# The recurrent rounds of an RWKV-7 and dilated-attention trunk: every PE step in 64x64 quadrants, and a new order of the steps after the fifth inverse level

## What is computed

```python
def step(state, inp):                       # per head of 64, 16 heads, 512 tokens
    r_t, w_t, k_t, v_t, a_t, b_t = inp
    sa = einsum('bhij,bhj->bhi', state, a_t)
    state = state * w_t + sa[..., None] * b_t + v_t[..., None] * k_t
    return state, einsum('bhij,bhj->bhi', state, r_t)
```

## Time and profile before

| | us |
|---|---|
| median of 3 runs | 1778.16 (1777.97 to 1778.27) |
| the profiled execution | 1777.27 |
| its span, first to last instruction | 1775.5 |
| PE busy | 1742.2 (98%) |
| weight loads busy | 1351.5 (76%) |
| DVE / ACT / POOL busy | 904.0 / 742.5 / 202.0 |
| granted PE clock | 1.0 throughout, save the first slice |
| rounds 0 to 7 of the recurrence | about 133 to 454 us from the start |

### The profile page before, as it was taken

One profiled execution on the slowest core, in us unless ns is written; L12 is line 12 of the kernel. 1 busy time (PEld: TensorE's weight loads), 2 busy tenths in 40 slices (PEclk: granted clock), 3 DMA queues, 4 the chain that ended last, 5 costly groups with the idle time before them and its releaser, 6 DMA issues.

```text
span 1775.5 us, 35844 instructions
## 1 busy us (share of the span) xinstructions
PE 1742.2 (98%) x15388; PEld 1351.5 (76%) x15388; DVE 904.0 (51%) x1567; ACT 742.5 (42%) x1285; POOL 202.0 (11%) x172
## 2 busy tenths in 40 slices
PE   7999999999999999999999999999999999999999
PEld 2746666666478888888888888888887788888887
DVE  6825555554454444333556656655656544444321
ACT  6434444432243222222565665565655532222211
POOL 0033344431100000000111111111110000000000
PEclk9999999999999999999999999999999999999999
DMA  4321222231133223333322222322222233333332
GB/s 128 99 64 61 88 68 68 66 104 62 60 96 95 95 95 96 106 95 95 104 81 89 84 83 73 85 82 83 84 84 72 72 95 95 95 98 101 98 95 95
DMA packets 58453, 155.00 MB, mean 87 GB/s; under 512 B 6503, under 2 KB 23447, under 8 KB 58296
## 3 DMA queue, kind: packets, MB, share of 16 engines
q1 hardware_dynamic: 58200, 152.63, 27.7%
q10 hardware_dynamic: 96, 0.07, 0.0%
HBM read 150.51 MB, written 11.61 MB: 91 GB/s over the span
## 4 chain that ended last, share of the span: by engine, by line
PE 92%; DVE 4%; ACT 2%; issue 1%; DMA 1%; POOL 1%; SPq 0%; ACTq 0%; DVEq 0%; POOLq 0%
PE bank L618 89%; PE bank L621 2%; DVE f L2278 1%; DVE f L2193 0%; DVE r L2107 0%; ACT f L1684 0%; ACT r L1369 0%; DMA f<-xT 0%; ACT f L1686 0%; DMA f<-stream 0%; DMA f<-const 0%; DVE r L1785 0%; DVE f L1796 0%; DVE f L1809 0%; DVE f L1837 0%
## 5 line engine op out<-in xcount | busy, mean ns | idle before, releaser
L618 PE MATMUL bank<-r 128*128 128x512 f32 x5424 | 1253.4, 391 | 2.4 <-DVE r L2107 1.0
L618 PEld LDWEIGHTS bank<-r 128*128 128x128 f32 x5424 | 1012.6, 188 | 221.2 <-issue 6.2
L618 PE MATMUL bank<-f 64*64 64x64 f32 (+6 forms) x9532 | 457.1, 279 | 24.8 <-issue 5.2
L1785 DVE TENSOR_TENSOR r<-f,r 128x1024 fp32r<-128x1024 f32 x222 | 283.9, 1279 | 362.6 <-ACT r L1369 362.3
L618 PEld LDWEIGHTS bank<-f 64*64 64x64 f32 (+3 forms) x9532 | 291.3, 138 | 183.7 <-issue 112.3
L1369 ACT ACTIVATE r<-f 128x1024 fp32r<-128x1024 f32 x222 | 232.4, 1048 | 146.3 <-PE bank L618 141.5
L2465 POOL TENSOR_TENSOR r<-f,r 128x512 fp32r<-128x512 f32 x48 | 66.9, 1394 | 807.6 <-ACT r L1673 807.6
L1652 ACT ACTIVATE r<-f 128x512 fp32r<-128x512 f32 x44 | 27.8, 632 | 215.6 <-DVE f L2146 215.6
L2176 DVE TENSOR_TENSOR f<-bank,f 128x512 f32<-128x512 f32 x72 | 56.1, 778 | 74.9 <-PE bank L618 72.2
L1684 ACT ACTIVATE f<-bank,f 128x512 f32<-128x512 f32 x48 | 33.0, 688 | 101.5 <-PE bank L618 100.8
L1649 ACT ACTIVATE f<-f 128x512 f32<-128x512 f32 x44 | 27.8, 632 | 110.5 <-DVE f L2136 110.5
(11 more groups left out here) (117 smaller groups left out, 926.2 us busy)
## 6 DMA issues: line engine op xcount, KB each, us to landing
f<-stream SPq DMA_DIRECT2D x246, 512.0 KB, 3.6
bias_copies<-bias_rows SPq DMA_DIRECT2D x6, 1536.0 KB
f<-xT SPq DMA_DIRECT2D x16, 256.0 KB, 4.4
f<-lora_out SPq DMA_DIRECT2D x16, 128.0 KB, 6.2
f<-bias_copies SPq DMA_DIRECT2D x64, 32.0 KB, 2.4
f<-bias_copies SPq DMA_DIRECT2D x32, 64.0 KB, 2.1
outT<-f SPq DMA_DIRECT2D x8, 256.0 KB, 4.5
f<-const SPq DMA_DIRECT2D x1, 576.0 KB, 3.7
```

What stands on the lines that cost most here:

```text
L618: return nc.tensor.matmul(out, lhsT, rhs, start=start, stop=stop, skip_group_check=True)
L1785: TT(r(lo_at(q), 1024), f(O_RAW + panel_of(q) % RAW * 1024, 1024), rf(hi_at(q), 1024), ALU.subtract).then_inc(s["w_lo"], 1)
```

## The change

PE's transposes and the value product become 64x64 products in all four quadrants (`flip_corners`), which go to banks 0 and 1 as one tensor `sides`, read by one ACT copy that spans both. Removal and b are flipped together, behind one signal. The variance sum moves from bank 0 to bank 7. All sixteen projection chunks are quartered. The order of PE's list after level 5 changes for rounds that have a pair behind them, and DVE's list with it. The core of the diff:

```diff
-        banks = [... psum_tensor(f"bank{i}", [P, 512], F32) for i in range(8)]
+        sides = ctx.enter_context(nc.psum_tensor("sides", [P, 1024], F32))
+        banks = [sides[:, 0:512], sides[:, 512:1024]]
+        banks += [... psum_tensor(f"bank{i}", [P, 512], F32) for i in range(2, 8)]
-        QUARTERED = (0, 3, 4, 6, 7, 9, 10, 11, 12, 13, 14, 15)
         def quartered(k, step):
-            return 0 <= k < NHP and step in QUARTERED
+            return 0 <= k < NHP
-        SIDE = {0: [("b_tr", 0), ("akv", 0), ("bonus", 1), ("var", -1),
+        SIDE = {0: [("v_tr", 0), ("b_tr", 0), ("akv", 0), ("k_tr", 0), ("bonus", 1),
                     ("first", 1), ("bsc", 1), ("ksc", 1), ("w", 2), ("g", -1)],
-                1: [("kk", 1), ("v_tr", 0), ("a_tr", 0), ("k_tr", 0), ("first", 1), ("bsc", 1), ("ksc", 1),
-                    ("a", 2)]}
+                1: [("kk", 1), ("first", 1), ("bsc", 1), ("ksc", 1), ("a", 2)]}
             def variance_ready(hp):
-                fill(0, "var", hp)
+                pe.wait_ge(s["y_sb"], hp + 1)
+            def flip_corners(at, off, by):
+                for q in range(NT):
+                    for e in range(2):
+                        for h in range(2):
+                            last = mm(banks[h][CH * e:CH * (e + 1), at + q * HD:at + (q + 1) * HD],
+                                      half(off(q) + e * CH, h), half(O_CON + by + h * HD, h))
+                return last
             def value_flip(hp):
-                for q in range(NT):
-                    last = mm(banks[1][:, q * P:(q + 1) * P], f(vin(hp) + q * P, P), con(C_CENTRE))
-                last.then_inc(s["v_tr"], 1)
+                flip_corners(0, lambda q: vin(hp) + q * P, C_CENTRE).then_inc(s["v_tr"], 1)
-            def removal_flip(hp):
...
-            def b_flip(hp):
...
+            def removal_and_b_flip(hp):
+                fill(0, "b_tr", hp)
+                pe.wait_ge(s["ar_a"], hp + 1)
+                flip_corners(0, lambda q: chunk(O_AR, hp, 2 * P, q, 0), C_ID)
+                pe.wait_ge(s["bt"], hp + 1)
+                flip_corners(4 * HD, lambda q: chunk(O_BT, hp, P, q, 0), C_ID).then_inc(s["b_tr"], 1)
             def k_flip(hp):
-                    last = flip(banks[1][:, q * P:(q + 1) * P], f(chunk(O_KT, hp, P, q, 0), P))
+                flip_corners(0, lambda q: chunk(O_KT, hp, P, q, 0), C_ID).then_inc(s["k_tr"], 1)
@@ PE's list @@
-                project(k, 8)
-                if here:
-                    next_inverse(k, 5)
-                    project(k, 9)
-                    solve(k)
-                if after:
-                    first_inverse(k + 1)
-                if not here:
-                    project(k, 9)
-                project(k, 10)
-                if here:
-                    transitions(k)
-                project(k, 11)
-                if after:
-                    b_scores(k + 1)
-                project(k, 12)
-                if here:
-                    readout(k)
-                if after:
-                    k_scores(k + 1)
-                project(k, 13)
+                if here and after:
+                    first_inverse(k + 1)
+                    next_inverse(k, 5)
+                    project(k, 8)
+                    solve(k)
+                    b_scores(k + 1)
+                    project(k, 9)
+                    transitions(k)
+                    project(k, 10)
+                    project(k, 11)
+                    readout(k)
+                    project(k, 12)
+                    k_scores(k + 1)
+                    project(k, 13)
+                elif here:
...
+            def flipped(at):
+                return sides[:, :].rearrange("p (h q n) -> p h q n", h=2, n=HD)[:, :, at * NT:(at + 1) * NT, :]
             def keep_removal(hp):
-                side(1, (s["a_tr"], hp + 1), bc(f(O_YY, 2 * S), (S, 2), (P, NT), (1, HD)),
-                     in_=banks[1][:, :].rearrange("p (q h n) -> p h q n", q=NT, h=2), scale=-1.0)
+                act.wait_ge(s["b_tr"], hp + 1)
+                A(bc(f(O_YY, 2 * S), (S, 2), (P, NT), (1, HD)), flipped(0), ACT.Copy, scale=-1.0)
             def keep_b(hp):
-                side(0, (s["b_tr"], hp + 1), f(O_BTOK))
+                side(0, (s["b_tr"], hp + 1), tokens(O_BTOK), in_=flipped(1))
@@ DVE's list @@
                     keep_inverse(k, 5)
-                    if k == NHP - 2:
-                        partial(3)
+                if after:
+                    first_masks(k + 1)
+                if here:
                     keep_solution(k)
                 if after:
-                    first_masks(k + 1)
+                    score_masks(k + 1, "bsc", O_BU)
+                if k == NHP - 2:
+                    partial(3)
                 if k == NHP - 1:
                     partial(6)
                 if here:
                     transitions(k)
                 if k == NHP - 3:
                     partial(0)
-                if after:
-                    score_masks(k + 1, "bsc", O_BU)
                 if here:
                     readout(k)
```

More of the change, by code:

```diff
@@ L254, in trunk @@
         ctx.enter_context(nc.sbuf_tensor("whole_map", [P, TOTAL], F32))
-        banks = [ctx.enter_context(nc.psum_tensor(f"bank{i}", [P, 512], F32)) for i in range(8)]
+        sides = ctx.enter_context(nc.psum_tensor("sides", [P, 1024], F32))
+        banks = [sides[:, 0:512], sides[:, 512:1024]]
+        banks += [ctx.enter_context(nc.psum_tensor(f"bank{i}", [P, 512], F32)) for i in range(2, 8)]
         bias_rows = nc.dram_tensor("bias_rows", [3 * 16 * 384], F32, kind="Internal").ap()
@@ L829, in value_flip @@
+            def value_flip(hp):
+                fill(0, "v_tr", hp)
+                if hp + 1 < NHP:
+                    side_read(pe, 1, "kk", hp + 1)
+                else:
+                    side_read(pe, 1, "ksc", hp)
                 if hp:
                     projection_kept(pe, proj_of_value(hp))
-                for q in range(NT):
-                    last = mm(banks[1][:, q * P:(q + 1) * P], f(vin(hp) + q * P, P), con(C_CENTRE))
-                last.then_inc(s["v_tr"], 1)
-            def removal_flip(hp):
-                fill(1, "a_tr", hp)
-                pe.wait_ge(s["ar_a"], hp + 1)
-                for q in range(NT):
-                    last = flip(banks[1][:, q * P:(q + 1) * P], f(chunk(O_AR, hp, 2 * P, q, 0), P))
-                last.then_inc(s["a_tr"], 1)
@@ L842, in b_flip @@
-            def b_flip(hp):
-                fill(0, "b_tr", hp)
+                flip_corners(0, lambda q: vin(hp) + q * P, C_CENTRE).then_inc(s["v_tr"], 1)
+            def removal_and_b_flip(hp):
+                fill(0, "b_tr", hp)
+                pe.wait_ge(s["ar_a"], hp + 1)
+                flip_corners(0, lambda q: chunk(O_AR, hp, 2 * P, q, 0), C_ID)
                 pe.wait_ge(s["bt"], hp + 1)
-                for q in range(NT):
-                    last = flip(banks[0][:, q * P:(q + 1) * P], f(chunk(O_BT, hp, P, q, 0), P))
-                last.then_inc(s["b_tr"], 1)
+                flip_corners(4 * HD, lambda q: chunk(O_BT, hp, P, q, 0), C_ID).then_inc(s["b_tr"], 1)
@@ L849, in k_flip @@
             def k_flip(hp):
-                fill(1, "k_tr", hp)
+                fill(0, "k_tr", hp)
                 pe.wait_ge(s["kt"], hp + 1)
-                for q in range(NT):
-                    last = flip(banks[1][:, q * P:(q + 1) * P], f(chunk(O_KT, hp, P, q, 0), P))
-                last.then_inc(s["k_tr"], 1)
+                flip_corners(0, lambda q: chunk(O_KT, hp, P, q, 0), C_ID).then_inc(s["k_tr"], 1)
             def first_inverse(hp):
@@ L859, in first_inverse @@
                     fill(h, "first", hp)
+                if hp:
+                    side_read(pe, 0, "k_tr", hp - 1)
                 pe.wait_ge(s["ar_a"], hp + 1)
@@ L1111, in _ @@
                 if here:
-                    off_diagonal(k, 5, (lambda q, h: sum_beside(0, O_Y, "var_ps", q, h)) if before else None)
+                    off_diagonal(k, 5, (lambda q, h: sum_beside(7, O_Y, "var_ps", q, h)) if before else None)
                 elif before:
-                    head_sum(0, O_Y, "var_ps")
-                project(k, 8)
-                if here:
+                    head_sum(7, O_Y, "var_ps")
+                if here and after:
[13 more added lines that the diff above has]
+                elif here:
+                    project(k, 8)
                     next_inverse(k, 5)
@@ L1559, in deviation @@
                     act.wait_ge(s["fin"], hp)
-                side(0, (s["var_ps"], hp + 1), f(O_RS), ACT.Ln, bias=kol(K_LNEPS), scale=1.0 / HD)
-                side_read(act, 0, "var", hp)
+                act.wait_ge(s["var_ps"], hp + 1)
+                A(f(O_RS), banks[7][:, :], ACT.Ln, bias=kol(K_LNEPS), scale=1.0 / HD).then_inc(s["var_ln"], 1)
+                act.wait_ge(s["var_ln"], hp + 1)
                 A(f(O_RS), f(O_RS), ACT.Exp, scale=-0.5).then_inc(s["y_rs"], 1)
```

17 lines of the change are left out of this document (10 added, 7 removed).

## The result

| | before | after |
|---|---|---|
| median | 1778.22 (1777.97 to 1780.74) | **1801.79** (1799.51 to 1805.42) |
| ratio, 95% interval | | 1.0131 (1.0112 to 1.015) |
| profiled execution / span | 1777.27 / 1775.5 | 1801.63 / 1799.8 |
| rounds 0 to 7 of the recurrence | 321.4 | 345.2 |
| the span behind them | 1321.4 | 1321.1 |

A forecast was written before the change was run, and what follows sets the result against it. PE, busy 98% of the span, was taken as the bound. Array, wait and one-time terms summed to -10.9 us, code loading added 4.8, giving -6.1 and 1772.1 us; range 1765 to 1781, the forecast's own 1767.5 to 1774.5.

The forecast's parts named there:

- The array terms: Rounds of the recurrence: quadrant flips, quartered chunks and new order gain 1.16 us per round net of readout's loss.
- code loading: Dense small products in the recurrence use up instruction packets before the next lands: +0.6 us per round, bounds 0 to 1.4.
- readout's wait: Before readout: less PE work covers the copies of the transitions, 1.72 us where 2.1 is needed; loss 0.4 per round.
- Walk 2 with value flip and chunk 1: Early stretch of each round: from 2.33 us to 1.52 as quadrant steps, gain 0.81.
- The 1.56 us for the first partial sum: Round 5: PE's wait for DVE's partial sum of output group 0 goes, -1.6 us once.
- A flip's 32 records: Each quadrant flip in the recurrence: sixteen products take 0.49 us; the 25 ns rule would make it 0.80.
- Rival 3: Packets become the clock: dense stretches without a chunk stall 0.7 us per packet, making it slower, 1784 us; chance 0.10.
- chunk 8's 0.19: After level 5: chunk 8, quartered, costs 0.86 us instead of 1.05, gain 0.19 per round.

The follow-up runs named there:

- e4: The changed kernel with the attention-bias copies (six of 1.5 MB in rounds 0 to 5) moved behind the recurrence as 48 small ones; 1787.1 us, ratio 1.003.
- e5: The kernel before with the attention-bias copies moved behind the recurrence as 48 small ones, PE's program unchanged; 1778.4 us, ratio 0.9975.
- e3: The kernel before with only the new order after level 5 and the variance sum in bank 7, no added matmuls; 1788.0 us, ratio 1.0036.
- e2: The kernel before with only all sixteen projection chunks quartered, 192 more matmul records; 1793.8 us, ratio 1.0062.
- e11: e4 with the value and k flips of the next pair moved behind readout, between chunks; 1798.2 us, ratio 1.0095.
- e7: The kernel before with 32 small products (128 instructions, half a packet) put once in front of everything; 1783.7 us, ratio 1.0007.
- e16: e12 with 32 small products (128 instructions, half a packet) put once in front of everything; 1782.5 us, ratio 1.0008.
- e8: The changed kernel with 32 small products (128 instructions, half a packet) put once in front of everything; 1803.7 us, ratio 1.0117.
- e10: The changed kernel with each flip as eight 64x128 products in two array halves instead of sixteen of 64x64; 1801.0 us, ratio 1.0118.
- e13: e11 with each flip as eight 64x128 products in two array halves; 1806.2 us, ratio 1.0142.
- e14: e4 with the ten weight panels of rounds 1 to 5 left out, so later projections use an old panel; 1785.4 us, ratio 1.0016.
- e12: The change without its flips (new order, all chunks quartered), with the attention-bias copies moved behind the recurrence; 1785.4 us, ratio 1.0024.
- e6: e4 with the recurrence's weight panels fetched in four parts of 128 KB each, released at four points of the round; 1788.9 us, ratio 1.0038.

## Why the prediction was wrong, point by point

**The array terms held.** The forecast was -1.16 per round without code loading, with +0.4 for readout's wait in it; rounds without stalls are 1.58 shorter. Walk 2 with value flip and chunk 1: 1.51 for 1.52. Readout starts 2.14 behind transitions (forecast 2.1), the last 0.20 of it a wait for DVE, in each of eight rounds (L1982 above). The 1.56 us for the first partial sum (rows 7) is gone. A flip's 32 records take 0.47 us, 15 ns each, as the row of b_scores had it. The page of the Trainium skill, "TensorE: Matmul & The Clock Gate", section "Wait - 56ns, not 53.3ns?", by which starts lie at least about 25 ns apart, is contradicted by this for quadrant products.

**The step that failed is "Code loading"**, +0.6 per round with bounds of 0 and 1.4. Stalls went from 1.87 to 7.09 per round, +5.2. Rival 3's mechanism was in the text (small products use up a packet before the next has landed), at 0.10, with 0.7 us per stall and 1784; what transfers do to it was not. Three things were wrong in the price:

1. The size of a stall. I took 0.7 from the stalls that I saw; after they last up to 2.7. The trace of before had the better number: two packets never start less than 3.42 us apart, while b_scores has 67 + 63 records in 0.98 us, so 256 instructions in 1.93. A dense stretch of one packet can thus stall by 3.4 - 1.9 = 1.5, and not by 0.7. A round of 9.5 packets needs 9.5 x 3.4 = 32 us at the least, of the 37.7 that it would last, and the little that is left is unevenly spread: a chunk runs through 16 records (8 of products, 8 of loads) in 0.86 us, a flip through 64 in half of that.
2. The transfers. Rows 3 and 4 have DMA shares up to 0.83 in the very stretches; I read them as nothing, since PE waits for no data there. e4 and e5 show what the copies do: 14.7 us to the new kernel and 2.6 to the old one. With copies and panels gone, the four rounds above are as long in the new kernel as in the old. A packet that starts late costs nothing where a chunk covers it, and 2 us or more where small products have used up the one before.
3. Rounds without added instructions. I scaled the stalls with the number of records. e3 adds none and has three times the waits.

**The tie that I didn't see** is e2's: chunk 8 quartered in the old order waits 1.7 us per round for `add_far`. In the whole change the order covers it, so it didn't spoil the sum, but I had counted chunk 8's 0.19 as a gain of the quartering alone.

**What adds up**: rounds 1 to 6 took 3.64 us more each (-1.58 in the array, +5.22 stalls), 21.8 us; rounds 0 and 7 the other 2.0. Of the stalls' 31 us in these six rounds, 22 are added waits for issue (25.5 against 3.5). The other 9 show as busy time or other waits; a stretch at half clock is among them (below), and the rest is not told apart.

I haven't tried the copies in other queues. Why e11 stalls no less though it is less dense is open too, and so is how much of e7's and e16's difference is the shift, and what starts a packet late where nothing else moves.

## What to carry to other kernels

Before PE's work is cut into smaller products, count its instructions in packets of 256 and hold every dense stretch against the shortest distance of two packets in the trace (3.3 to 3.4 us here): what runs through a packet faster than that is given back as stalls. Price such a stall from that distance, and look at what bulk transfers run beside it: in the four rounds compared here density alone gave back the whole saving, and the transfers made a loss of it. Moving them out of the dense stretches gave more (e5, -0.25%) than any change of the products. A saving in the array of 4% of a round isn't a saving in time until the instructions for it arrive.

## What the runs showed of the hardware that was not expected

- Instruction packets: 3.3 us apart at the least. PE mostly goes on 2.2 to 3.0 us after a packet's start. In the kernel after, a packet starts 1.1 us after PE's entry into the one before with under 20 KB moved in between, and 2.0 with over 400 KB (medians of 40 and 18 packets, with exceptions both ways).
- The clock can fall at such a wait. Behind the 2.70 us wait of 185.45 the granted clock was 1.2 GHz (0.5) for 3.4 us, from 186.7 on:

```profile
185.50:189.00 3.50, 3.50 (x109) 2.50 (x111) 1.54 (x3) 1.32 (x4) 1.17 (x2) 0.67 0.02 5
```

  One or two stretches like it are in e3, e8, e10, e11, e13 and e14, none in the recurrence of before, e5 and e12. Each of the eight stands at a wait for issue of 1.9 to 2.9 us; but waits of 2.4 in e6 and 2.2 in e8 passed without one. So a long stall can cost its length and then part of what follows.
- Products of 64x128 in two halves of the array show no overlap (0.13 us each, 1.04 for the eight of a flip), those of 64x64 in four quadrants do (16 in 0.47).
